# Two-at-a-time splits of the operands of seven-product chunks, with their sums made in DRAM by accumulating transfers

## Reference

```python
for layer in range(DEPTH):            # DEPTH = 2
    h = rms_norm(x, norm_mix_g[layer])
    ...                               # layer 0: 16 heads with forget gates; layer 1: 8 heads with shared keys and values
    x = x + mixer
    x = x + sq_relu_mlp(rms_norm(x, norm_ffn_g[layer]), ffn_w_up[layer], ffn_w_down[layer])

def sq_relu_mlp(h, w_up, w_down):
    return jnp.square(jax.nn.relu(h @ w_up)) @ w_down      # 1024 -> 4096 -> 1024
```

## Time and profile before

| | us |
|---|---|
| median of 3 runs (lowest to highest) | 1981.71 (1980.32 to 1981.88) |
| the profiled execution | 1981.71 |
| its span in the trace | 1980.0 |
| PE busy | 1961.3 (99%) |
| PE weight loads busy | 1640.2 (83%) |
| VectorE (DVE) busy | 1341.7 (68%) |
| ScalarE (ACT) busy | 894.3 (45%) |
| GpSimd (POOL) busy | 60.4 (3%) |

### The profile page before, as it was taken

One profiled execution on the slowest core, in us unless ns is written; L12 is line 12 of the kernel. 1 busy time (PEld: TensorE's weight loads), 2 busy tenths in 40 slices (PEclk: granted clock), 3 DMA queues, 4 the chain that ended last, 5 costly groups with the idle time before them and its releaser, 6 DMA issues.

```text
span 1980.0 us, 29280 instructions
## 1 busy us (share of the span) xinstructions
PE 1961.3 (99%) x10404; PEld 1640.2 (83%) x10404; DVE 1341.7 (68%) x2145; ACT 894.3 (45%) x1417; POOL 60.4 (3%) x114
## 2 busy tenths in 40 slices
PE   9999999999999999999999999999999999999999
PEld 7777789898987887898988788778888888888888
DVE  6555579687777776797787769574444686563545
ACT  4555554445444554544444443474333544432333
POOL 0000000000110110000001100000000000000000
PEclk9999999999999999999999999999999999999999
DMA  4332243323562114523226513211322412223232
GB/s 158 86 85 85 75 148 129 106 79 98 184 205 78 52 49 157 179 69 106 96 99 214 190 46 104 74 64 65 96 96 98 151 43 85 96 95 105 88 99 91
DMA packets 61292, 209.05 MB, mean 106 GB/s; under 512 B 7160, under 2 KB 10232, under 8 KB 61200
## 3 DMA queue, kind: packets, MB, share of 16 engines
q1 hardware_dynamic: 49920, 168.32, 25.8%
q0 software_dynamic: 10560, 37.28, 6.0%
q10 hardware_dynamic: 720, 2.23, 0.3%
HBM read 205.66 MB, written 2.13 MB: 105 GB/s over the span
## 4 chain that ended last, share of the span: by engine, by line
PE 94%; DVE 4%; ACT 1%; DMA 1%; issue 1%; SPq 0%; DVEq 0%; ACTq 0%
PE bank L893 23%; PE bank L895 23%; PE bank L894 23%; PE bank L1216 4%; PE bank L1218 4%; PE bank L1217 4%; PE bank L1016 1%; PE bank L1091 1%; PE bank L1075 1%; PE bank L998 1%; PE bank L1001 1%; PE bank L1043 1%; PE bank L949 1%; PE bank L951 1%; PE bank L950 1%
## 5 line engine op out<-in xcount | busy, mean ns | idle before, releaser
L893 PE MATMUL bank<-b_hi,w_hi 128*128 128x512 f32 x2060 | 813.0, 395 | 6.6 <-DVE w_lo L2764 4.0
L895 PE MATMUL bank<-b_hi,w_lo 128*128 128x512 f32 x2060 | 802.9, 390 | 0.0
L894 PE MATMUL bank<-b_lo,w_hi 128*128 128x512 f32 x2060 | 802.7, 390 | 0.0
L893 PEld LDWEIGHTS bank<-b_hi,w_hi 128*128 128x128 f32 x2060 | 387.2, 188 | 95.9 <-issue 8.2
L895 PEld LDWEIGHTS bank<-b_hi,w_lo 128*128 128x128 f32 x2060 | 387.0, 188 | 81.0
L894 PEld LDWEIGHTS bank<-b_lo,w_hi 128*128 128x128 f32 x2060 | 387.4, 188 | 80.2 <-issue 2.4
L2764 DVE TENSOR_TENSOR w_lo<-w_raw,w_hi 128x1024 fp32r<-128x1024 f32 (+3 forms) x259 | 306.8, 1185 | 210.2 <-ACT w_hi L1810 209.5
L1810 ACT ACTIVATE w_hi<-w_raw 128x1024 fp32r<-128x1024 f32 (+3 forms) x259 | 265.5, 1025 | 263.3 <-PE bank L895 253.6
L3916 DVE SCALAR_TENSOR_TENSOR arena<-bank,vec,arena 128x511 f32<-128x511 f32 x88 | 65.7, 749 | 85.8 <-ACT arena L2658 80.5
L1216 PE MATMUL bank<-parts,w_hi 128*128 128x256 f32 x384 | 108.7, 283 | 3.3 <-DVE x L3113 3.3
L1218 PE MATMUL bank<-parts,w_lo 128*128 128x256 f32 x384 | 107.9, 281 | 0.0
(11 more groups left out here) (398 smaller groups left out, 2537.9 us busy)
## 6 DMA issues: line engine op xcount, KB each, us to landing
w_raw<-in_wstream SPq DMA_DIRECT2D x253, 512.0 KB, 3.5
arena<-in_ada POOLq DMA_DIRECT2D x48, 512.0 KB, 4.3
plain<-in_wseven SPq DMA_DIRECT2D x24, 512.0 KB, 5.0
early<-in_wseven SPq DMA_DIRECT2D x24, 512.0 KB, 6.8
w_raw<-in_wstream SPq DMA_DIRECT2D x12, 384.0 KB, 3.0
arena<-crow POOLq DMA_DIRECT2D x16, 256.0 KB, 4.8
w_raw<-in_wstream SPq DMA_DIRECT2D x10, 256.0 KB, 2.6
x<-in_xT ACTq DMA_DIRECT2D x4, 512.0 KB, 6.6
```

The costliest lines, as they stand in the source:

```text
L893: nc.tensor.matmul(dst, whi, rhs_hi(k), start=(k == 0), stop=False)
L894: nc.tensor.matmul(dst, whi, rhs_lo(k), start=False, stop=False)
L895: last = nc.tensor.matmul(dst, wlo, rhs_hi(k), start=False, stop=(k == n - 1))
```

## The change

The splits of a chunk are made for two products at a time (a "pair" p, 14 per chunk, 1024 columns), through three places: `w_hi[0]`/`w_lo[0]`, columns 2 and 3 of `b_hi[2]`/`b_lo[2]`, and `w_hi[1]`/`w_lo[1]`. The raw data of a pair comes from two loads of 256 KB into one of four places. VectorE's adds are gone: SP loads all seven operands, three from `wseven` and four from a new DRAM tensor `seven_sums`. POOL makes that tensor ahead: a turn (`sum_turn`) works on two units at a time in four steps, each a turn behind the one before: copy the units (2 MB), add pieces 1 and 2 to columns 0 and 1 (1 MB), add column 0 to column 2, add column 2 to column 3 (0.5 MB each). A turn first waits until all transfers of the turns before have landed. A layer has 12 units, so 6 such pairs of units and 9 turns: in the first attention layer turn 0 ahead of the loop over pairs, turns 1 to 6 behind the rows of pairs 2 to 7, 7 and 8 behind them; in the second turn h behind head h's L844, turn 8 behind the last. SP waits for a layer's sums ahead of its first chunk's loads, POOL in the first layer also ahead of L816. The two last panels' splits at a chunk's end become one whole and two halves.

```diff
...
+        PANELS = SEVEN * QUAD // 2
+        RAW = 4
+        PIECE = (0, None, None, 3, None, None, 2)
+        SUM_AT = (None, 1, 2, None, 0, 3, None)
+        UNITS = QUAD * SEVEN_CHUNKS
...
+        sum_in, SUM_STEP = crow_out, 2
+        SUM_TURNS = UNITS // SUM_STEP + 3
...
+            def load_seven(i):
+
+                p = i // 2
+                if p >= RAW and i % 2 == 0:
+                    sp.wait_ge(seven_lo, seven_count(p - RAW))
+                n, o = i // SEVEN, i % SEVEN
+                src, at = (seven_rows, PIECE[o]) if PIECE[o] is not None else (sum_rows, SUM_AT[o])
+                sp.dma_start(seven_raw(p)[:, i % 2 * T:(i % 2 + 1) * T], src[n * P:(n + 1) * P, at * T:(at + 1) * T])\
+                  .then_inc(seven_in[p % RAW], 16)
...
                     if c == 0:
 
                         sp.wait_ge(free, count)
+                        sp.wait_ge(sum_in, sum_count(run))
...
+            def sum_turn(run, turn):
+
+                first, n = seven_first(run) // SUM_STEP, UNITS // SUM_STEP
+                pool.wait_ge(sum_in, SUM0[run] + 16 * sum(min(max(turn - back, 0), n) for back in range(4)))
+                for back, (to, src, at) in enumerate(((slice(0, 4 * T), seven_rows, slice(0, 4 * T)),
+                                                      (slice(0, 2 * T), seven_rows, slice(T, 3 * T)),
+                                                      (slice(2 * T, 3 * T), sum_rows, slice(0, T)),
+                                                      (slice(3 * T, 4 * T), sum_rows, slice(2 * T, 3 * T)))):
+                    if 0 <= turn - back < n:
+                        units = slice((first + turn - back) * SUM_STEP * P, (first + turn - back + 1) * SUM_STEP * P)
+                        if back:
+                            pool.dma_start(sum_rows[units, to], src[units, at], accum_op=ALU.add).then_inc(sum_in, 16)
+                        else:
+                            pool.dma_start(sum_rows[units, to], src[units, at]).then_inc(sum_in, 16)
...
+            sum_turn("ff_a", 0)
+            for p in range(2, FOX_PAIRS):
+
+                pool.wait_ge(row_min, 6 * p - 6)
+                rows(p, p % 2)
+                sum_turn("ff_a", p - 1)
+            for turn in range(FOX_PAIRS - 1, SUM_TURNS):
+                sum_turn("ff_a", turn)
...
+            for h in range(MLA_HEADS):
+                m = h % 2
+                pool.wait_ge(rope_hi, h + 3)
+                pool.tensor_tensor(qr_part[1][m], q_rope[m], qr_part[0][m].bitcast(F32), ALU.subtract).then_inc(rope_lo, 1)
+                sum_turn("ff_b", h)
+            for turn in range(MLA_HEADS, SUM_TURNS):
+                sum_turn("ff_b", turn)
...
-                        pe.wait_ge(seven_lo, seven_count(i))
+                        pe.wait_ge(seven_lo, seven_count(i // 2))
...
+                    for p in range(PANELS - 3):
+                        act.wait_ge(seven_mm, MM0 + 2 * (at + p) + 2)
+                        high(at + p + 3)
...
+                def low(p):
+                    dve.wait_ge(seven_hi, seven_count(p))
+                    dve.tensor_tensor(seven_slot(seven_w_lo, p), seven_raw(p), seven_slot(seven_w_hi, p).bitcast(F32),
                                       ALU.subtract).then_inc(seven_lo, 1)
...
-                        if i + 3 < end:
-                            low(at + 3)
-                        else:
-                            w_half(c, first, i + 3 - end)
-                        if i % SEVEN == 0:
-                            four(at // SEVEN)
-                        if i % SEVEN == 2 and i + 5 < end:
-                            two(at // SEVEN + 1)
-                        if i % SEVEN == 4 and i + 3 < end:
-                            three(at // SEVEN + 1)
+                        if i % 2 == 0 and i // 2 + 2 < PANELS:
+                            low(at // 2 + 2)
+                        if i == end - 4:
+                            w_second(c, first)
+                        if i in (end - 3, end - 2):
+                            w_half(c, first, i - end + 3)
...
```

More of the change, by code:

```diff
@@ L373, in program, with seven_raw, seven_count, seven_slot @@
         ff_s = [ar(8), ar(9)]
[L377 to L391, removed]
+        PANELS = SEVEN * QUAD // 2
[3 more added lines that the diff above has]
+        UNITS = QUAD * SEVEN_CHUNKS
+        def seven_raw(p):
+            return (plain if p % RAW < 2 else early)[:, 4 + 2 * (p % 2):6 + 2 * (p % 2), :].rearrange("p a t -> p (a t)")
+        def seven_count(p):
+            return LO0 + p + 1 + 2 * (p // PANELS)
+        seven_w_hi, seven_w_lo = ([w[0], b[2][:, 2:4, :].rearrange("p a t -> p (a t)"), w[1]] for w, b in ((w_hi, b_hi), (w_lo, b_lo)))
+        def seven_slot(w, p):
+            return w[p % PANELS % 3][:, 0:PANEL]
         SEVEN_RUNS = ("ff_a", "ff_b")
@@ L740, in load_ffn @@
                         sp.wait_ge(free, count)
+                        sp.wait_ge(sum_in, sum_count(run))
                     if c < SEVEN_CHUNKS:
-                        for q in range(QUAD):
-                            load_seven(QUAD * seven_chunk(run, c) + q)
+                        end = SEVEN * QUAD
+                        for i in range(end):
+                            load_seven(end * seven_chunk(run, c) + i)
                 load_panels(at, KT)
@@ L2109, in up_tiles @@
                 def up_tiles(first, n, c):
+                    p0 = PANELS * seven_chunk(run, c)
                     for j in range(first, first + n):
-                        if j + 2 < first + n:
+                        left = first + n - 1 - j
+                        if left >= 2:
                             w_split(j + 2)
@@ L2114, in up_tiles @@
                             act.wait_ge(mm_done, t0 + j + 1)
-                            for i in range(2):
-                                high(SEVEN * QUAD * seven_chunk(run, c) + 2 * (j + 2 - first - n) + i)
+                            high(p0 + 2 * (1 - left))
                         square(j)
+                        if left == 1:
+                            high(p0 + 1)
                         if j % 2 and j < first + n - 1:
@@ L3068, in w_split, with w_second @@
                     split((g0 + j) // 2, j % 2)
+                def w_second(c, first):
+                    dve.wait_ge(seven_hi, seven_count(PANELS * (seven_chunk(run, c) + 1) - 1) + 1)
+                    dve.tensor_tensor(w_lo[1][:, 0:PANEL], w_raw[1][:, 0:PANEL], w_hi[1][:, 0:PANEL].bitcast(F32), ALU.subtract)\
+                       .then_inc(seven_lo, 1)
                 def w_half(c, first, u):
[L3072 to L3076 removed]
@@ L3093, in three @@
-                def three(n):
-                    dve.wait_ge(seven_add, ADD0 + 3 * n + 1)
-                    dve.tensor_tensor(seven_raw(n, 2), seven_raw(n, 0), seven_raw(n, 1), ALU.add).then_inc(seven_add, 1)
-                def four(n):
-                    dve.wait_ge(seven_add, ADD0 + 3 * n + 2)
-                    dve.tensor_tensor(seven_raw(n, 5), seven_raw(n, 2), seven_raw(n, 3), ALU.add).then_inc(seven_add, 1)
+                    cols = slice(u * T, (u + 1) * T)
+                    if u:
+                        dve.wait_ge(w_hi_done, g0 + first + 2)
+                    else:
+                        dve.wait_ge(seven_hi, seven_count(PANELS * (seven_chunk(run, c) + 1) - 1) + 2)
@@ L3163, in up_tiles @@
                             w_split(j + 2)
-                        elif last:
-                            low(SEVEN * QUAD * seven_chunk(run, c) + 2)
-                        else:
-                            n0 = QUAD * seven_chunk(run, c)
-                            two(n0)
-                            low(SEVEN * n0)
-                            low(SEVEN * n0 + 1)
-                            three(n0)
+                        else:
+                            low(PANELS * seven_chunk(run, c) + last)
                         if not last:
```

91 lines of the change are left out of this document (35 added, 56 removed).

## The result

The change makes the kernel slower: 2025.43 us (median of 4 runs, 2023.79 to 2026.45) against 1981.8 (4 runs), a ratio of 1.022 with a 95% interval of 1.0202 to 1.0237. Forecast was 2039 us by this mechanism.

The account below looks back on a forecast made before the run. PE, busy 1961.3 of 1980.0 us, was taken as the bound, so only its waits count. 1981.71 - 3.5 (chunks) + 61 (late condition row behind POOL's turns) = 2039 us, range 1977 to 2140.

Parts of the forecast that it names:

- The bound and the place: Whole kernel: PE bounds; the loss is PE waiting before second-layer logits for POOL's subtraction, queued behind turns.
- The chunks, -3.5: Six chunks by seven products: product 6's stall goes in four, about 0.6 us stays at product 11; 3.5 us gained.
- The chunks do not gain: Rival, chunks: stall only moves or pieces land late, 0 instead of -3.5; shifts every case under 4 us, no chance given.
- The price of a turn, 28.5 with its issue: POOL's queue: full turn 27.4 us, one pass per copy, two per add, plus 1.1 issue.
- the fixed 3.0: POOL's turns: fixed 3.0 us added to each turn's transfer time, rounded up from 2.6 on this queue's loads.
- The walk of the heads: Second attention layer: subtractions held from head 4, 7 us late; head 6 37, head 7 53, condition row 61 late.
- The end of the layer: Second attention layer's end: VectorE stands on the condition row, so the last 8 us count too in 61 us late.
- Taken as nothing, and nothing: First attention layer, SP's issues and wait, ScalarE, chunk ends, stream of pieces: each forecast to cost nothing.
- Panel loads beside them take longer, nothing: Panel loads beside turns: longer, but split only two panels (some 16 us) after issue, so no cost.
- The rule against the change: Skill pages, for turns: copies at 214 GB/s, reductions at half; full turn 39 us, sum about 2105 us.
- VectorE's 58 us: VectorE, whole kernel: busy time forecast about 70 us less with its adds removed.

Follow-up runs that it names:

- turns alone: Kernel before, with all turns and their waits added on POOL, the sums read by nobody and VectorE's adds kept: 2032.93 us, ratio 1.0255.
- chunks alone: Changed kernel without turns and their waits; SP loads plain quarters in place of sums, sums of weights left out: 1977.76 us, ratio 0.9975.
- plain copies: Changed kernel with the three accumulating transfers of a turn made plain copies of the same bytes, additions left out: 1991.24 us, ratio 1.0044.
- copies alone: Changed kernel with only the copies left in the second layer's turns, their three additions left out: 1978.18 us, ratio 0.998.
- turns earlier: Changed kernel, second layer's turns 0 to 2 ahead of the layer, 3 to 6 behind odd heads, 7 and 8 later: 1986.5 us, ratio 1.0022.
- the last two runs: Kernel before with only the order of operations in the chunks changed, no DRAM sums, two such orders: 1978.53 us and 1979.1 us.
- the run that had less work and the better order: Changed kernel without turns, sums of weights left out, `sums_low` moved from behind product 8 to behind product 9: 1974.93 us, ratio 0.9965.

## Why the prediction was right, and where its sizes were off

- **The bound and the place.** Right: the loss is PE waiting ahead of the logits, released by POOL's subtraction, behind turns that POOL waits for. The turns alone give it whole; turns of 8.7 us in the same places give nothing.
- **The chunks, -3.5.** Right: -3.4 by starts in the changed kernel, 3.0 to 6.7 by the run of the chunks alone. The stall at product 6 went, and 0.59 us stayed at product 11 where 0.6 was walked. "The chunks do not gain" falls.
- **The price of a turn, 28.5 with its issue.** This is the term that was mis-sized: 25.8, 25.5 and 23.3 were measured, and 9.2 for turn 7 where 12.2 stood. Issue to issue, turns 0 to 7 took 157.2 us (644.93 to 802.15) where the walk had 175.1. The transfers themselves were sized well: the three full turns took 20.2, 21.8 and 21.3 us of all engines, where one pass for the copy and two for the adds made 20.0. Within that the copy was lighter (5.8 us, not 6.7) and the adds heavier (15.7, not 13.4), but with the factor of two between an add and a copy. Too large were the terms put around them. The panel stream beside a full turn held 0.159, 0.105 and 0.006 of the engines, not 0.18, since a PE that waits uses no panels. And the fixed 3.0 with the issue of 1.1 stood for 4.1 us, where the engines were idle for some 1.4 a turn (21.1, 2.3 for the panel stream and 1.4 make the 24.9 to within 0.1); the copy's issue took 0.55 us, not 1.1.
- **The walk of the heads.** Right in kind: pairs of subtractions became single ones a turn apart. The first wait of PE came with head 5, not 4: turn 3 went at 697.72, early enough for head 4. Counted from a layer that starts 1.7 us earlier (the two chunks before it), head 6 is 25.4 us late, not 37, and the condition row, at 802.71, 42.6 late, not 61: 18.4 too much.
- **The end of the layer.** The walk took the row's own transfer as before. It landed some 9.9 us after its issue, where it was 4.7 before: turn 8's add of 0.52 MB had gone out on the same queue 0.6 us ahead. The run of the turns alone has that add ahead too, and 9.7 us; the runs of plain copies, of copies alone and of turns earlier have no transfer of a turn right ahead, and 4.7, 4.7 and 4.6. These 5.2 us were not in the sum. Two errors, 18.4 too much and 5.2 too little, take 2039 to 2025.8, against 2025.43. A walk with this term in it would have said 2044; leaving it out brought the forecast nearer by luck.
- **Taken as nothing, and nothing:** the first attention layer (rows of the last pair at 173.56 against 173.69, cvec at 229.25 well ahead of its use), SP's issues, ScalarE, the chunk's ends, the wait that SP got, the wider stream of pieces (3.8 us to landing). "Panel loads beside them take longer, nothing" nearly holds where the turns stand: PE has 0.5 us less in the first layer, and in the second head 2's subtraction, which waits for no turn, is at 673.59 against 671.93 in the run of copies alone, 1.7 us late. Moved ahead of the second layer three turns cost 5 us, and all nine beside chunks some 40.
- **The rule against the change.** By the pages a full turn was 39 us and the time 2105. Copies ran above their figure, 362 GB/s at full share. On adds the trace agrees with "Collectives: The Full Stack", The bandwidth ceiling (the Trainium skill), by which a reduction needs two source reads and runs at half of a copy: 15.7 us of all engines against 8.0 for the same bytes.
- **VectorE's 58 us.** Forecast as 70 less. The 3.5 us did not need them: the last two runs get as much with all of that work still there. The rest of the stalls (0.56 us a chunk, 2.2 in all) went only in the run that had less work and the better order, 7.1 us below the kernel before; whether order alone could get it was not tried.

## What to carry to other kernels

Before work is moved off an engine that isn't the bound, look at whether its share of a stall is work or order: here the same 3.5 us came from putting four operations of VectorE and one of ScalarE some products later, at no cost. A queue that also feeds the critical path must not wait for bulk transfers between two of its deadlines: compare the length of one wait with the spacing of what is queued behind it, since 8.7 us in a 13.5 us step were free and 25 us cost 44. Total DMA time is a second budget: transfers moved to where no engine waits for their issuer still delay every load they run beside, so put them beside the stage that asks for the fewest bytes.

## What the runs showed of the hardware

- A copy of 2.10 MB from DRAM to DRAM took 8.7 us, 242 GB/s with everything counted and 362 at full share of the engines. Three smaller transfers of 2.10 MB together took 8.0 us of all engines as copies and 15.7 as adds, so adding doubles a transfer's price.
- The length of a load depends on what it shares the engines with: a piece of 256 KB lands in 3.8 us at a DMA share of 0.55, in 12.5 at 0.98.
- POOL's subtraction has 2.30 us right behind a turn's issues and 1.28 by itself, in the same kernel (rows at 725.77 and 702.04). In the run of plain copies it has 1.31 right behind a turn's issues (at 709.71), so the longer time goes with accumulating ones. Its row begins before the issues' end (724.64 + 2.15), so part of it may be issuing.
- TensorE's granted clock was 0.77 of 2.4 GHz over 725 to 750, where PE was busy 14.3 of 25 us, and 1.00 in the first attention layer and in the chunk. It mixes stretches at either level; the first logits matmul behind an 11.19 us wait took 0.79 us where it takes 0.48 at full clock, and the next ones start 0.43 us apart (754.42, 754.85) where it is 0.23 in the kernel before (741.23, 741.46). So a stall costs more than its own length, here 6.5 us of PE's busy time beside some 39 of waiting.
